# Differential attention in a two-block transformer kernel: rope from PSUM, a scaling on ScalarE, units at uneven distances

## The chip, the cores and the metric

The kernel runs on one core of a Trainium2 chip. The metric is the device time in microseconds (us); it is stated as the median of several executions. One further execution was recorded by the hardware profiler. All views of the trace below are of that execution.

## What is computed

Two transformer blocks run one after the other, in fp32, on 512 tokens of width 1024. The change touches only the even mixer of the second block, and in it the differential attention: 8 heads, each with two maps of 64 features, whose softmaxes are subtracted.

```python
def diff_attention_group(q, k, v, pos, layer, lambdas, subln):
    q = rope(q.reshape(bsz, s, 2 * hh, d), pos).reshape(bsz, s, hh, 2, d)
    k = rope(k.reshape(bsz, s, 2 * hh, d), pos).reshape(bsz, s, hh, 2, d)
    lam = jnp.exp(jnp.sum(lf[0] * lf[1])) - jnp.exp(jnp.sum(lf[2] * lf[3])) + lam_init
    scale = d ** -0.5                      # 1/8
    def block(start, q1b, q2b):            # 128 queries against all keys, chunk-causal mask
        p1 = masked_softmax(einsum('bqhd,bkhd->bhqk', q1b, k1) * scale, mask)
        p2 = masked_softmax(einsum('bqhd,bkhd->bhqk', q2b, k2) * scale, mask)
        return einsum('bhqk,bkhe->bqhe', p1 - lam * p2, vf)
    o = rms_norm(o, subln) * (1.0 - lam_init)
```

## The kernel before

**Stages.** The kernel is written by hand, engine by engine; every engine runs its instructions strictly in the order of the program and waits on semaphores. The stage of the change is `ev_qk_out`, about 1595 to 1865 us. On every engine it is a loop over 192 steps. TensorE makes in steps 0 to 127 the 16 projections of queries and keys (`ev_qk`, 8 steps each: n, k = divmod(step, 8)) and in steps 128 to 191 the first halves of the 8 output tiles (`ev_out`). Each step is one product: three matmuls of 128x512 (high x high, high x low, low x high parts of fp32), lines 939 to 941. All the other work stands between products, at steps given by functions.

**Rope.** When projection n is done, ScalarE copies it from its PSUM bank (n % 2) to `raw2` (line 2179, k = 0 of the next tile). At k = 2 TensorE exchanges its halves with a permutation matrix into bank 2 (`swap`, line 1466), and VectorE multiplies the copy by the cosines (line 2904), the exchanged one by the sines (2906) into `swp`, and adds (2907) into `qk2`; this posts `roped`.

**Units.** A unit is one head and one block of 128 queries, with 128, 256, 384 or 512 keys (i = 0 to 3): 32 units, the four of a head one after another, 4 steps apart from step 40 on (`UNIT_AT`, `UNIT_STEPS`). For the unit that starts at step s:

- s: TensorE `scores` (1477) for both maps into banks 4 and 5. VectorE `maxes`: masks a corner (2915), takes the maximum (2917), multiplies it by -1/8 (2918). ScalarE `exps` (2139), two exponentials with their sums. VectorE `weights` of the unit before: reciprocals of the sums (2925), second map times its inverse sum and -lambda (2927), first map times its inverse sum plus the second (2928). It stands in the order of the program behind `maxes` of the new unit.
- s + 8 (`TURN`): TensorE transposes the weights (`turn`, 1487) into bank 6, ScalarE copies them (2148).
- s + 11 (`MIX`): TensorE multiplies by the values (`mix`, 1497) into bank 7.

**Heads.** At `head_mixed_at(h)`, the step of the last mix, VectorE copies the head's output (2972) and ScalarE squares it (2188); the next head's first `mix` waits for that copy. Three steps on, TensorE sums the squares (`sub_sum`, 1507). After heads 3 and 7, at + 4, VectorE makes variance and reciprocal (2977, 2978) and ScalarE four roots (`sub_root`, 2156), and from `spread_at(h)` on TensorE spreads them (`sub_rows`, 1518) and VectorE scales (2982); ScalarE and VectorE split the result into high and low parts (2193, 2939). In steps 120 to 129 they also split the eight tiles of the mamba branch's y (2201, 2959).

**Beside it** GpSimd splits each weight panel, once in 16 steps, into a high part (3354, 4 pieces) and a low part (3358, 4 pieces). SyncE loads the panels and, once all 16 tiles are roped, x (line 860).

## Time and profile before

| | |
|---|---|
| median of 3 executions | 2912.23 us (2909.16 to 2913.40) |
| profiled execution | 2908.97 us |
| its span in the trace | 2907.1 us |
| busy: TensorE, VectorE, ScalarE, GpSimd | 97%, 48%, 29%, 47% of the span |
| mean granted TensorE clock | 0.988 of full |

The profile says of each engine how long it was busy, and of each instruction when it began, how long it lasted, and which instruction of another engine released it when it had stood still ahead of it. Matmuls overlap, and their ends are modelled: the distance from start to start is the measure, not the duration. Times in the trace count from the span's start.

### The profile page before, as it was taken

The page shows a single profiled execution, that of the slowest core. Times are in us where ns is not written, and L with a number is a line of the kernel's source. Part 1 is how long each engine was busy: PE and PEld are TensorE (multiplying, and loading weights), DVE is VectorE, ACT ScalarE, POOL GpSimd, SP SyncE. Part 2 cuts the span into 40 slices and gives each one's busy share as a digit, 9 for nine tenths or more (in the row PEclk, how much of TensorE's full clock was granted, in tenths as well). Part 3 has the DMA queues.
Part 4 walks back from the last instruction along what each step waited for, and adds up shares of the span by engine and source line. Part 5 has one row for each costly group of instructions (what it writes and reads, how often), then busy time and mean ns, then how long its engine had stood idle before and what let it go on. Part 6 is the DMA issues. An engine that isn't in the chain of part 4 may idle for free.

```text
span 2907.1 us, 36763 instructions
## 1 busy us (share of the span) xinstructions
PE 2810.6 (97%) x14588; PEld 2171.8 (75%) x14588; DVE 1397.8 (48%) x2266; ACT 847.4 (29%) x1575; POOL 1355.7 (47%) x1106
## 2 busy tenths in 40 slices
PE   7999999999989999999999989999999998999997
PEld 5888777777878877677886656778788755788886
DVE  3321556776573122435847777523825856511113
ACT  3011432331130133322336234232223234222222
POOL 2344323324434654558765543754544412744443
PEclk8999999999999999999999999999999999999999
DMA  7112222222321122123311112222333320323322
GB/s 269 44 44 66 66 66 95 70 70 94 131 76 59 58 73 73 62 91 122 105 61 59 58 48 69 84 94 87 102 96 90 116 64 30 126 91 89 99 85 74
DMA packets 244837, 243.81 MB, mean 84 GB/s; under 512 B 5392, under 2 KB 234640, under 8 KB 244048
## 3 DMA queue, kind: packets, MB, share of 16 engines
q1 hardware_dynamic: 243376, 237.96, 25.6%
q0 software_dynamic: 1312, 3.80, 0.5%
q8 instruction: 102, 1.67, 0.2%
q14 instruction: 47, 0.39, 0.0%
HBM read 233.22 MB, written 7.34 MB: 83 GB/s over the span
## 4 chain that ended last, share of the span: by engine, by line
PE 83%; DVE 11%; issue 2%; ACT 2%; POOL 1%; SPq 1%; DMA 1%; DVEq 0%; POOLq 0%; ACTq 0%
PE psum L939 22%; PE psum L941 21%; PE psum L940 21%; PE psum L1209 4%; PE psum L1188 1%; PE psum L1144 1%; DVE columns L2644 1%; PE psum L1164 1%; PE psum L1326 1%; PE psum L1143 1%; POOL columns L3358 1%; PE psum L1213 1%; DVE columns L2917 1%; PE psum L1477 1%; SPq L776 1%
## 5 line engine op out<-in xcount | busy, mean ns | idle before, releaser
L939 PE MATMUL psum<-columns,columns 128*128 128x512 f32 (+1 forms) x3464 | 1348.6, 389 | 13.4 <-POOL columns L3358 5.0
L941 PE MATMUL psum<-columns,columns 128*128 128x512 f32 (+1 forms) x3464 | 1263.6, 365 | 0.0
L940 PE MATMUL psum<-columns,columns 128*128 128x512 f32 (+1 forms) x3464 | 1262.5, 364 | 0.0
L3358 POOL TENSOR_TENSOR columns<-columns,columns 128x512 fp32r<-128x512 f32 (+1 forms) x676 | 912.1, 1379 | 437.8 <-ACT columns L1873 404.6
L3354 POOL TENSOR_TENSOR columns<-columns,columns 128x512 fp32r<-128x512 f32 x392 | 419.1, 1100 | 1005.7 <-PE psum L941 775.3
L939 PEld LDWEIGHTS psum<-columns,columns 128*128 128x128 f32 x3464 | 654.6, 189 | 198.9 <-issue 77.1
L940 PEld LDWEIGHTS psum<-columns,columns 128*128 128x128 f32 x3464 | 655.3, 189 | 125.7 <-issue 28.6
L941 PEld LDWEIGHTS psum<-columns,columns 128*128 128x128 f32 x3464 | 653.8, 189 | 112.5
L1873 ACT ACTIVATE columns<-columns 128x1024 fp32r<-128x1024 f32 (+2 forms) x154 | 136.8, 936 | 171.9 <-PE psum L941 166.2
L2644 DVE SCALAR_TENSOR_TENSOR columns<-columns,columns,columns 128x256 f32<-128x256 f32 x224 | 154.4, 743 | 0.0
L2626 DVE SCALAR_TENSOR_TENSOR columns<-columns,psum 128x512 f32<-128x512 f32 x80 | 54.8, 685 | 187.5 <-PE psum L1209 185.0
L3026 DVE TENSOR_TENSOR columns<-columns,psum 128x512 f32<-128x512 f32 x44 | 30.3, 689 | 207.7 <-PE psum L941 207.7
L1209 PE MATMUL psum<-columns,columns 128*128 128x512 f32 x256 | 121.2, 596 | 1.9 <-DVE columns L2603 1.9
L3020 DVE TENSOR_TENSOR columns<-psum,columns 128x512 f32<-128x512 f32 x44 | 30.3, 692 | 152.3 <-PE psum L941 152.0
L2585 DVE TENSOR_REDUCE columns<-psum 128x1 f32<-128x768 f32 (+3 forms) x80 | 61.5, 769 | 64.5 <-PE psum L1144 63.4
L3142 DVE TENSOR_TENSOR psum<-psum,columns 128x512 f32<-128x512 f32 x32 | 22.4, 700 | 129.7 <-PE psum L941 129.6
L1984 ACT ACTIVATE columns<-psum,columns 128x768 f32<-128x768 f32 (+3 forms) x80 | 59.3, 742 | 71.6 <-DVE columns L2588 71.6
L2214 ACT ACTIVATE columns<-columns 128x512 fp32r<-128x512 f32 x44 | 27.8, 633 | 179.5 <-DVE columns L3026 179.5
L1999 ACT ACTIVATE columns<-psum 128x512 f32<-128x512 f32 (+1 forms) x80 | 44.0, 550 | 113.4 <-PE psum L1164 113.4
L2025 ACT ACTIVATE columns<-psum,columns 128x512 f32<-128x512 f32 x64 | 43.6, 681 | 113.8 <-PE psum L941 113.7
L1991 ACT ACTIVATE columns<-columns,columns 128x768 f32<-128x768 f32 (+3 forms) x80 | 62.6, 783 | 46.0 <-DVE columns L2596 45.9
L2210 ACT ACTIVATE columns<-columns 128x512 f32<-128x512 f32 x44 | 27.8, 634 | 162.5 <-DVE columns L3020 162.2
(414 smaller groups left out, 2745.6 us busy)
## 6 DMA issues: line engine op xcount, KB each, us to landing
columns<-in_w_merge SPq DMA_DIRECT2D x32, 1024.0 KB, 6.7
columns<-in_w_ada SPq DMA_DIRECT2D x24, 1024.0 KB, 5.7
columns<-in_w_in SPq DMA_DIRECT2D x22, 1024.0 KB, 5.3
columns<-in_ev_w_in SPq DMA_DIRECT2D x22, 1024.0 KB, 5.2
columns<-in_ffn_gate SPq DMA_DIRECT2D x22, 1024.0 KB, 5.4
columns<-in_ffn_up SPq DMA_DIRECT2D x22, 1024.0 KB, 5.3
columns<-in_ffn_down SPq DMA_DIRECT2D x16, 768.0 KB, 4.7
columns<-in_ffn_down SPq DMA_DIRECT2D x16, 640.0 KB, 4.3
```

Of the source, the lines that this page charges most:

```text
L939: mm(dst, weights(0, k), moving(0, k), start=start and k == 0, stop=False)
L940: mm(dst, weights(0, k), moving(1, k), start=False, stop=False)
L941: last = mm(dst, weights(1, k), moving(0, k), start=False, stop=stop and k == k_tiles - 1)
L1209: last = mm(psum[:, o:o + SEQ], brs[:, n % 2, k, part * P:(part + 1) * P], gx[:, r, k, :], start=k == 0, stop=k == 1)
L1873: last = f(w_parts[0][:, (SPLITS[q] - 1) % 2, a:b], ring[:, raw_slot, a:b], ACT.Copy)
L1984: f(prob[:, u % 2, 0:n], psum[:, o:o + n], ACT.Exp, bias=cols[:, u % 2:u % 2 + 1], scale=0.125, accum_out=cols[:, 4 + u % 2:5 + u % 2]).th ...
L1991: f(prob[:, u % 2, 0:n], prob[:, u % 2, 0:n], ACT.Identity, scale=cols[:, 24 + u % 8:25 + u % 8]).then_inc(prob_weighed, 1)
L2585: order(v.tensor_reduce(top, psum[:, o:o + n], AX.X, ALU.max))
L2626: v.scalar_tensor_tensor(out=acc if j < quarter else g, in0=g, scalar=1.0, in1=y, op0=ALU.add, op1=ALU.mult).then_inc(merge_used, 1)
L2644: last = v.scalar_tensor_tensor(out=acc, in0=w, scalar=sil[:, k, b:b + 1], in1=acc, op0=ALU.mult, op1=ALU.add)
L3354: last = g.tensor_tensor(high[:, c], raw[:, c], zero.broadcast_to([P, c.stop - c.start]), ALU.add)
L3358: last = g.tensor_tensor(low[:, c], raw[:, c], high[:, c].bitcast(F32), ALU.subtract)
```

## The change

Within the stage, six things:

1. The rope's cosine product becomes `cosines`, one step after the raw copy (k = 1), and reads the projection in its PSUM bank; the swap and the rest of the rope move from k = 2 to k = 4 (`ROPE_AT`). The sine product is written back into bank 2, and the sum reads it there; the buffer `swp` goes. So a projection's bank is free for the next but one only when its tile is roped: TensorE waits for `roped` where it waited for `raw_ready`.
2. The factor 1/8 goes from the exponential into the raw copy and the cosine product, for query tiles only (`is_query`).
3. The maximum is written negated by the reduction itself; the multiplication behind it goes.
4. `weights` is parted: `inverses` (reciprocals and -lambda times that of the second map) ahead of `maxes`, and behind it the one combining instruction, which waits for ScalarE. ScalarE's new `scale` multiplies the second map by its column.
5. Units start at 0, 3, 7 and 11 of each head's 16 steps instead of 0, 4, 8 and 12, from step 40 on; ScalarE's exponentials are put 2 steps after the start in its order (`EXPS`), `turn` and `mix` stay at 8 and 11.
6. The work at a head's end moves back against `head_mixed_at`: the copy from + 0 to + 2, the square from + 0 to + 3, `sub_sum` from + 3 to + 5, variance and roots from + 4 to + 6, `sub_rows` from + 7 to + 9. `head_mixed_at(h)` itself is one step earlier.

```diff
--- before.py
+++ after.py
@@ -297,7 +297,8 @@
 V_SLOTS, Z_SLOTS, HEADS_AT = 16, 16, 12
 QK_STEPS, OUT_STEPS = 128, 64
 UNITS2 = [(h, i) for h in range(8) for i in range(4)]
-UNIT_AT, UNIT_STEPS, TURN, MIX = 40, 4, 8, 11
+UNIT_STARTS = [40 + 16 * h + (0, 3, 7, 11)[i] for h, i in UNITS2]
+ROPE_AT, EXPS, TURN, MIX, LAST_WEIGHTS = 4, 2, 8, 11, UNIT_STARTS[-1] + 5
 
 
 def qk_tile(n):
@@ -305,20 +306,24 @@
     return 2 * (n // 4) + n % 2 + 8 * (n % 4 // 2)
 
 
+def is_query(n):
+
+    return n % 4 < 2
+
+
 def unit2_at(step, phase):
 
-    u = step - UNIT_AT - phase
-    return u // UNIT_STEPS if u >= 0 and u % UNIT_STEPS == 0 and u // UNIT_STEPS < len(UNITS2) else None
+    return UNIT_STARTS.index(step - phase) if step - phase in UNIT_STARTS else None
 
 
 def head_mixed_at(h):
 
-    return UNIT_AT + UNIT_STEPS * (4 * h + 3) + MIX
+    return UNIT_STARTS[4 * h + 3] + MIX
 
 
 def spread_at(h):
 
-    return head_mixed_at(3) + 7 + 3 * h if h < 4 else head_mixed_at(7) + 7 + 2 * (h - 4)
+    return head_mixed_at(3) + 9 + 3 * h if h < 4 else head_mixed_at(7) + 9 + 2 * (h - 4)
 
 
 OD_TILES = (4, 5, 6, 7, 8, 9, 0, 1, 2, 3)
@@ -524,7 +529,7 @@
         lamw, lam_products = take(128, at=A + 19952), take(2, 64, at=A + 20080)
 
         qk2 = take(16, SEQ, at=A + 10240)
-        swp, raw2 = take(SEQ, at=4096), take(2, SEQ, at=5120)
+        raw2 = take(2, SEQ, at=5120)
         sq5, rs5 = take(2, SEQ, at=0), take(SEQ, at=2 * SEQ)
         pr_diff = (take(2, 2, SEQ, at=brs_at), take(2, SEQ, at=A + 4096))
         sub_sq, sub_rs, sub_v = take(SEQ, at=A + 5120), take(SEQ, at=A + 5120 + SEQ), take(P, at=A + 18448)
@@ -1527,10 +1532,10 @@
                         mix(u)
                     if step % 2 == 0 and 1 <= step // 2 <= KD:
                         gate_sum(step // 2 - 1)
-                    if k == 2 and 1 <= n <= 16:
+                    if k == ROPE_AT and 1 <= n <= 16:
                         swap(n - 1)
                     for h in range(8):
-                        if step == head_mixed_at(h) + 3:
+                        if step == head_mixed_at(h) + 5:
                             sub_sum(h)
                         if step == spread_at(h):
                             sub_rows(h)
@@ -1544,17 +1549,15 @@
                             if n < 2:
                                 pe.wait_ge(z_ready, 7 + n)
                             else:
-                                pe.wait_ge(raw_ready, n - 1)
+                                pe.wait_ge(roped, n - 1)
                         o, src = n % 2 * BANK, h2_parts
                     else:
                         t = n - 16
                         if k == 0:
                             if t % 2 == 0:
                                 w = split_ready(PANEL0["ev_out"] + t // 2)
-                            if t < 2:
-                                pe.wait_ge(raw_ready, 15 + t)
-                            elif t == 2:
-                                pe.wait_ge(roped, 16)
+                            if t < 3:
+                                pe.wait_ge(roped, min(15 + t, 16))
                             else:
                                 pe.wait_ge(half_added, t - 2)
                         if t == 0:
@@ -2136,9 +2139,15 @@
                         act.wait_ge(turned2, u - 1)
                     for a in range(2):
                         o, c = (4 + a) * BANK, 2 * (u % 2) + a
-                        last = f(pr_diff[0][:, u % 2, a, 0:n], psum[:, o:o + n], ACT.Exp, bias=cols[:, c:c + 1], scale=0.125,
+                        last = f(pr_diff[0][:, u % 2, a, 0:n], psum[:, o:o + n], ACT.Exp, bias=cols[:, c:c + 1],
                                  accum_out=cols[:, 4 + c:5 + c])
                     last.then_inc(p2_ready, 1)
+
+                def scale(u):
+                    n = (UNITS2[u][1] + 1) * P
+                    p = pr_diff[0][:, u % 2, 1, 0:n]
+                    act.wait_ge(total_inverted, UNITS0[2] + u + 1)
+                    f(p, p, ACT.Identity, scale=cols[:, 5 + 2 * (u % 2):6 + 2 * (u % 2)]).then_inc(prob_weighed, 1)
 
                 def copy(u):
                     n = (UNITS2[u][1] + 1) * P
@@ -2158,6 +2167,11 @@
 
                 for step in range(QK_STEPS + OUT_STEPS):
                     n, k = divmod(step, 8)
+                    u = unit2_at(step, 0)
+                    if u:
+                        scale(u - 1)
+                    if step == LAST_WEIGHTS:
+                        scale(len(UNITS2) - 1)
                     u = unit2_at(step, TURN)
                     if u is not None:
                         copy(u)
@@ -2176,17 +2190,17 @@
                         act.wait_ge(gemm_done, JOB0["ev_qk"] + i + 1)
                         if i >= 2:
                             act.wait_ge(roped, i - 1)
-                        f(raw2[:, i % 2, :], psum[:, i % 2 * BANK:(i % 2 + 1) * BANK], ACT.Copy).then_inc(raw_ready, 1)
-                    u = unit2_at(step, 0)
+                        f(raw2[:, i % 2, :], psum[:, i % 2 * BANK:(i % 2 + 1) * BANK], ACT.Copy, scale=0.125 if is_query(i) else 1.0).then_inc(raw_ready, 1)
+                    u = unit2_at(step, EXPS)
                     if u is not None:
                         exps(u)
                     for h in range(8):
-                        if step == head_mixed_at(h):
+                        if step == head_mixed_at(h) + 3:
                             act.wait_ge(o2_used, h + 1)
                             if h:
                                 act.wait_ge(sub_summed, h)
                             f(sub_sq, qk2[:, h, :], ACT.Square).then_inc(sub_squared, 1)
-                        if h % 4 == 3 and step == head_mixed_at(h) + 4:
+                        if h % 4 == 3 and step == head_mixed_at(h) + 6:
                             sub_root(h // 4)
                         if step == spread_at(h) + 1:
                             act.wait_ge(sub_scaled, h + 1)
@@ -2898,13 +2912,16 @@
 
             def ev_qk_out():
 
+                def cosines(n):
+                    dve.wait_ge(raw_ready, n + 1)
+                    order(v.scalar_tensor_tensor(out=qk2[:, qk_tile(n), :], in0=psum[:, n % 2 * BANK:(n % 2 + 1) * BANK],
+                                                 scalar=0.125 if is_query(n) else 1.0, in1=cosd, op0=ALU.mult, op1=ALU.mult))
+
                 def rope(n):
-                    x = qk2[:, qk_tile(n), :]
-                    dve.wait_ge(raw_ready, n + 1)
-                    v.tensor_tensor(x, raw2[:, n % 2, :], cosd, ALU.mult)
+                    x, swp = qk2[:, qk_tile(n), :], psum[:, 2 * BANK:3 * BANK]
                     dve.wait_ge(swapped, n + 1)
-                    order(v.tensor_tensor(swp, psum[:, 2 * BANK:3 * BANK], sind, ALU.mult))
-                    v.tensor_tensor(x, x, swp, ALU.add).then_inc(roped, 1)
+                    order(v.tensor_tensor(swp, swp, sind, ALU.mult))
+                    v.tensor_tensor(x, swp, x, ALU.add).then_inc(roped, 1)
                     dve.wait_ge(roped, n + 1)
 
                 def maxes(u):
@@ -2914,17 +2931,20 @@
 
                     order(v.memset(s[0:64, :, n - 64:n], NEG))
                     c = cols[:, 2 * (u % 2):2 * (u % 2) + 2]
-                    order(v.tensor_reduce(c, s[:, :, 0:n], AX.X, ALU.max))
-                    v.tensor_scalar(c, c, -0.125, None, ALU.mult).then_inc(maxed2, 1)
-
-                def weights(u):
-
-                    n = (UNITS2[u][1] + 1) * P
+                    v.tensor_reduce(c, s[:, :, 0:n], AX.X, ALU.max, negate=True).then_inc(maxed2, 1)
+
+                def inverses(u):
                     c = cols[:, 4 + 2 * (u % 2):6 + 2 * (u % 2)]
                     dve.wait_ge(p2_ready, u + 1)
                     order(v.reciprocal(c, c))
+                    v.tensor_scalar(c[:, 1:2], c[:, 1:2], lamw[:, 5:6], None, ALU.mult).then_inc(total_inverted, 1)
+
+                def weights(u):
+
+                    n = (UNITS2[u][1] + 1) * P
+                    c = cols[:, 4 + 2 * (u % 2):6 + 2 * (u % 2)]
                     p = pr_diff[0][:, u % 2, :, 0:n]
-                    order(v.tensor_scalar(p[:, 1], p[:, 1], c[:, 1:2], lamw[:, 5:6], ALU.mult, ALU.mult))
+                    dve.wait_ge(prob_weighed, UNITS0[2] + u + 1)
                     v.scalar_tensor_tensor(out=p[:, 0], in0=p[:, 0], scalar=c[:, 0:1], in1=p[:, 1], op0=ALU.mult, op1=ALU.add)\
                         .then_inc(p2_weighted, 1)
 
@@ -2957,20 +2977,25 @@
                         i = step - QK_STEPS + KD - 2
                         dve.wait_ge(y_high, i + 1)
                         v.tensor_tensor(y_parts[1][:, i, :], xbc[:, i, :], y_parts[0][:, i, :].bitcast(F32), ALU.subtract).then_inc(y_split, 1)
-                    if k == 2 and 1 <= n <= 16:
+                    if k == 1 and 1 <= n <= 16:
+                        cosines(n - 1)
+                    if k == ROPE_AT and 1 <= n <= 16:
                         rope(n - 1)
                     u = unit2_at(step, 0)
                     if u is not None:
+                        if u:
+                            inverses(u - 1)
                         maxes(u)
                         if u:
                             weights(u - 1)
-                    if step == UNIT_AT + UNIT_STEPS * len(UNITS2):
+                    if step == LAST_WEIGHTS:
+                        inverses(len(UNITS2) - 1)
                         weights(len(UNITS2) - 1)
                     for h in range(8):
-                        if step == head_mixed_at(h):
+                        if step == head_mixed_at(h) + 2:
                             dve.wait_ge(mixed2, 4 * h + 4)
                             v.tensor_copy(qk2[:, h, :], psum[:, 7 * BANK:8 * BANK]).then_inc(o2_used, 1)
-                        if h % 4 == 3 and step == head_mixed_at(h) + 4:
+                        if h % 4 == 3 and step == head_mixed_at(h) + 6:
                             dve.wait_ge(sub_summed, h + 1)
                             if h == 7:
                                 dve.wait_ge(sub_std, 1)
```

## Rows read from the trace of the kernel before

**Rows 1.** The page, part 1: busy us, share of the span, instructions.
```profile
PE 2810.6 (97%) x14588; PEld 2171.8 (75%) x14588; DVE 1397.8 (48%) x2266; ACT 847.4 (29%) x1575; POOL 1355.7 (47%) x1106
```

**Rows 2.** TensorE's waits, 1590 to 1860 us: total us, times, longest.
```profile
PE psum L1487 <- DVE columns L2928: 12.4, 13, 2.1
PE psum L1518 <- ACT columns L2156: 2.9, 1, 2.9
...
PE psum L1477 <- ACT columns L2139: 1.2, 1, 1.2
PE psum L1466 <- ACT columns L2179: 1.1, 1, 1.1
```

**Rows 3.** TensorE in time: start, us, instruction, [idle before it, releaser].
```profile
1708.98 0.27 PE L1487 MATMUL psum<-columns,columns 128*128 128x128 f32 x1
1709.18 0.92 PE L1477 MATMUL psum<-columns 64*128 64x384 f32 x4
...
1714.31 0.40 PE L941 MATMUL psum<-columns,columns 128*128 128x512 f32 x1
1714.95 0.44 PE L1487 MATMUL psum<-columns,columns 128*128 128x128 f32 x2 [0.24 <-DVE columns L2928]
...
1721.29 0.55 PE L1487 MATMUL psum<-columns,columns 128*128 128x128 f32 x3 [1.42 <-DVE columns L2928]
...
1731.56 0.27 PE L1487 MATMUL psum<-columns,columns 128*128 128x128 f32 x1
...
1769.88 0.33 PE L1487 MATMUL psum<-columns,columns 128*128 128x128 f32 x1 [2.10 <-DVE columns L2928]
```

**Rows 4.** VectorE and GpSimd in time, 1709 to 1720 us.
```profile
1709.22 4.03 POOL L3354 TENSOR_TENSOR columns<-columns,columns 128x512 fp32r<-128x512 f32 x4 [12.38 <-PE psum L941]
...
1710.40 0.96 DVE L2917 TENSOR_REDUCE columns<-psum 128x2 f32<-128x768 f32 x1
1711.39 0.89 DVE L2918 TENSOR_SCALAR columns<-columns 128x2 f32<-128x2 f32 x1
...
1713.33 6.09 POOL L3358 TENSOR_TENSOR columns<-columns,columns 128x512 fp32r<-128x512 f32 x4
...
1713.43 1.46 DVE L2928 SCALAR_TENSOR_TENSOR columns<-columns,columns 128x256 f32<-128x256 f32 x1
```

**Rows 5.** By line: ns least/median/most, first and last start, forms.
```profile
L2904 DVE TENSOR_TENSOR columns<-columns,columns x16: 679/688/1753, 1602.6 to 1771.4; 128x512 f32<-128x512 f32 x16
L2906 DVE TENSOR_TENSOR columns<-psum,columns x16: 677/680/692, 1605.9 to 1772.0; 128x512 f32<-128x512 f32 x16
L2907 DVE TENSOR_TENSOR columns<-columns,columns x16: 691/868/1339, 1606.6 to 1772.7; 128x512 f32<-128x512 f32 x16
L2918 DVE TENSOR_SCALAR columns<-columns x32: 169/170/1065, 1636.1 to 1815.7; 128x2 f32<-128x2 f32 x32
L2928 DVE SCALAR_TENSOR_TENSOR columns<-columns,columns x32: 351/684/1465, 1640.5 to 1818.5; 128x128 f32<-128x128 f32 x8, 128x256 f32<-128x256 f32 x8, 128x384 f32<-128x384 f32 x8, 128x512 f32<-128x512 f32 x8
```

**Rows 6.** ScalarE: group of 1040 to 1250 us by shape; one square in time.
```profile
L1991 ACT ACTIVATE columns<-columns,columns 128x512 f32<-128x512 f32 x5 | 3.6, 720 | 0.1
...
1709.21 0.63 ACT L2188 ACTIVATE columns<-columns 128x512 f32<-128x512 f32 x1 [1.62 <-DVE columns L2972]
```

**Rows 7.** The roots of the first four heads, in time.
```profile
1741.23 0.95 DVE L2978 RECIPROCAL columns<-columns 128x128 f32<-128x128 f32 x1
1742.21 1.26 ACT L2156 ACTIVATE columns<-columns 32x128 f32<-32x128 f32 x4 [4.78 <-DVE columns L2978]
1743.53 2.07 PE L1518 MATMUL psum<-columns,columns 128*128 128x512 f32 x2 [2.89 <-ACT columns L2156]
```

**Rows 8.** Two stretches: us, busy us (instructions) by engine, granted clock, DMA.
```profile
1743.50:1747.00 3.50, 3.47 (x8) 2.15 (x9) 2.20 (x6) 3.47 (x7) 0.00 (x0) 0.52 0.83 286
...
1770.20:1773.70 3.50, 3.50 (x11) 1.82 (x10) 3.36 (x5) 0.39 (x1) 0.76 (x1) 0.58 0.00 0
```

**Rows 9.** VectorE in time: a scaling with one operand in PSUM.
```profile
1751.11 0.74 DVE L2982 SCALAR_TENSOR_TENSOR columns<-columns,columns,psum 128x512 f32<-128x512 f32 x1
```

4 lines of the change are left out of this document (2 added, 2 removed).

## Prediction

> **What bounds the kernel now.** Read the page's first part before anything else: TensorE is busy for 97% of the span, every other engine for under half of it [rows 1]. So an edit on VectorE or ScalarE can only give back time in which TensorE stood still in this stage, and the next view is TensorE's waits over the stage (1590 to 1860 us), line by line [rows 2]. The largest is line 1487, the transposes of `turn`, which waited for line 2928, the last instruction of `weights` on VectorE: 12.4 us in 13 waits. Three single waits follow: 2.9 us of `sub_rows` (1518), 1.2 us of `scores` (1477), 1.1 us of `swap` (1466).
>
> Third view, TensorE in order of time through one head [rows 3]. Matmuls of 512 columns start about 0.23 us apart and are modelled to last 0.40, so the real loss of a wait is its idle time plus about 0.17: the last product before a turn started at 1714.31, the turn at 1714.95 instead of 1714.54. The same two turns are late in each head: that of the second unit (0.24 here) and that of the third (1.42). One head (first turn to first turn, 1708.98 to 1731.56) takes 22.6 us, of which (0.24 + 0.17) + (1.42 + 0.17) = 2.0 is waiting. 20.6 us is TensorE's own work and stays.
>
> Why is `weights` late? Between 1709 and 1722 GpSimd splits the next weight panel, 4 pieces of 1.0 us and then 4 of 1.5 [rows 4]. In that burst the 2-column negation 2918 took 0.89 us against a median of 0.17, and the 256-column line 2928 took 1.46, more than the 0.684 median over all widths. By line over the whole stage [rows 5]: 2904 and 2907, both of whose inputs lie in SBUF, range from 0.68 to 1.75 and from 0.69 to 1.34; 2906, which reads PSUM, is 0.677 to 0.692 in all 16 cases. This is the part of VectorE's time that the change goes at.
>
> **The clock.** The granted clock averaged 0.52 and 0.58 of full in two stretches of 3.5 us [rows 8], that is mostly at the lower of its two levels, 1.2 instead of 2.4 GHz. The first began as the 2.89 us wait of 1518 ended [rows 7], the second after the 2.10 us wait at 1769.88 [rows 3]. Each costs 3.5 x (1 - 0.52) = 1.7 and 3.5 x (1 - 0.58) = 1.5 us. Waits of 1.42 us are not followed by one.
>
> **All that can be won**: turns 12.4 + 13 x 0.17 = 14.6; `sub_rows` 3.1; `swap` 1.3; `scores` 1.4; clock 3.2. Together 23.6 us.
>
> **Part by part.** *Rope reads PSUM.* Today 2904 + 2906 + 2907 are 0.69 + 0.68 + 0.87 by the medians and 1.75 + 0.68 + 1.07 where they fall into the burst. `cosines` becomes a scalar_tensor_tensor with one PSUM operand; the nearest row is 2982, 0.74 [rows 9]. The other two read and write a PSUM bank; nearest 2906, 0.68. In-place PSUM output isn't shown among my rows: from below 0.68, from above 0.87 (2907), I take 0.69. New sum 2.1 us, the same in and out of the burst: 0.1 to 1.4 us less of VectorE per tile, 16 tiles. `cosines` also waits for the raw copy, so two engines never read the bank together; the bank is now free only when the tile after it is roped. That is the wait `roped` at k = 0 on TensorE: rope of tile n-2 stands at step 8(n-1)+4, four steps (4 x 0.7 = 2.8 us and more with the unit work) ahead. I cost it at nothing; if VectorE were over 3 us late at that point it would appear.
> *Scale in the copy and in `cosines`*: immediates of instructions that are there anyway, nothing.
> *Negated maximum*: removes 32 x 2918 (0.17, up to 1.07 in the burst), 12 us of VectorE, directly on the chain scores, maximum, exponential.
> *Second map scaled on ScalarE*: VectorE loses 32 x 2927 and keeps the reciprocal, plus a one-column multiplication that can wait for a GpSimd piece like 2918 did (0.17 to 1.07). ScalarE gets 32 scalings; the same operation with a column as scale stands in the first block, line 1991, 0.72 us at 512 columns [rows 6], so some 2 us per head on an engine with 29% load [rows 1]. Behind it in ScalarE's queue are the copy of the transposes and the raw copy; both have a step or more of room. VectorE waits for it in `weights`, but runs `maxes` in between, which hides it.
> *Starts at 0, 3, 7, 11 of 16 steps, swap at k = 4.* `weights(u)` still stands at the next unit's start. Second unit: its turn now comes 4 steps after, and the rope, 2.2 to 3.5 us of VectorE, no longer stands in between. Third unit: 4 steps, the rope behind `weights`. I laid the rows out for one head (scores of the third unit start at t = 0): scores to end of the maximum takes from 1709.18 to 1711.36, 2.2 us [rows 3, 4]; `weights` of the second unit then waits up to 1.0 for a GpSimd piece and takes about 0.5, done by 3.3 to 3.7; its turn comes at scores 0.92 + four products of 0.70 (three matmuls 0.23 apart) + the first unit's turn 0.20 = 3.9 [rows 3]. Cleared, with 0.2 to 0.6 to spare. In the same way the third unit's turn has over 1 us, the fourth's over 1. So the 14.6 us of the turns go.
>
> **What is late next.** *The head's sum of squares.* In program order VectorE copies the last head's output after `weights` of the second unit (0.68), ScalarE squares it (0.63 [rows 6]), and `sub_sum` stands on TensorE right behind this turn and the mix: t = 3.9 + 0.4 (two transposes, rows 3's 0.44) + 0.2 (one matmul of 128 columns, like one transpose) = 4.5. The chain gives 3.4 + 0.68 + 0.63 + 0.1 for the hand-over = 4.8. New wait about 0.3 per head, bounds 0 (weights meets no piece) and 1.0 (it meets a piece of 1.5). Five ordinary heads: 1.5 us (0 to 5).
> *Head 5* (steps 120 to 135) has the eight low halves of y (two SBUF inputs, 0.68 to 1.75 like 2904) and two of the four 0.74 us subnorm scalings ahead of that copy. Extra 0.68 to 1.5 + 0.74, plus about 1 us of backlog: `mix` and `sub_sum` wait 1.6 to 4, I take 2.5. Before, this stretch lost 1.3 + 2.3.
> *Head 6*: the low half of head 3 now lies just ahead of the copy (step 144 both), in the burst: 0.5 + 0.68 more, 1.5 us in all.
> *Group root*: `sub_sum` to `sub_rows` is 4 steps as before; rope, the 0.95 us reciprocal and the 1.26 us of roots [rows 7] still come one after another, and now the fourth unit's exponentials queue behind the roots with a table load. I find 1.6 to 2.4 us at `sub_rows` and 1.1 at the next `scores`: 3.1, unchanged, and so is its low clock, 1.7.
> *First scores*: one step less between the first two units, but a rope that is 1 us shorter: 1.4, unchanged (0.5 to 2.5).
> *Second stretch of low clock*: its waits shrink from 3.6 to about 2.5; half a chance, 0.8.
> Sum lost after: 1.5 + 2.5 + 1.5 + 3.1 + 1.7 + 1.4 + 0.8 = 12.5. Gain 23.6 - 12.5 = **11.1 us**. The reload of x (waits for the last rope) and the weight panels follow TensorE and have room; the rest of the kernel runs the same.
>
> **A rule weighed against the rows.** Line 2906 never felt the GpSimd burst, 2904 and 2918 did [rows 5]. The Trainium skill (SBUF — State Buffer, Who interferes with whom) says that a VectorE instruction contends with GpSimd when it has two SBUF inputs or is in a two-port mode, which tensor_scalar can enter, and not with at most one SBUF input outside those modes. By that rule, the trace agrees for the parts removed, but it also speaks against the change: `weights` keeps two SBUF inputs and the small multiplication in `inverses` is a tensor_scalar, so both stay exposed.
>
> **Rivals.** (1) *All goes*: the root and both low-clock stretches as well, new waits near nothing; only the first scores stay and some 2 us. For it: VectorE gets some 3 us per head free. Against it: the root's chain is as long. Gain 17 to 22 us, about 2893. Chance 0.12. (2) *Turns stay partly late*: the 0.2 to 0.6 us of the second unit is thin; if `weights` misses it by 0.7 in each head, 8 x 0.7 = 5.6 come back, and gain is 3 to 7, about 2907. Chance 0.17 (0.07 of it still beyond 0.2%). (3) *The new waits eat it*: `sub_sum` at its bound of 1.0 in five heads, head 5 at 4 with its low clock: 5 + 4 + 1.5 (head 6) + 1.5 (clock) + 4.8 (root with its clock) + 1.4 = 18.2, a gain of 5.4 at the most and less with any turn late: about 2909 and no change that can be told. Chance 0.10. (4) *Slower*: ScalarE and VectorE now wait for each other twice per unit in program order. If the copy of the head's output with its square falls behind a GpSimd piece of 1.5 us and the late scaling, `mix` and `sub_sum` wait over 2.5 us in each of 7 heads, 17 us, and each such wait may bring a low clock of 1.5. It decides from (23.6 - 9.5) / 7 = 2.0 us per head, where 9.5 is root 4.8, first scores 1.4, clock 0.8 and 2.5 for what heads 5 and 6 have extra; at 3.0, with one more low clock, 7 x 3.0 + 9.5 + 1.5 - 23.6 = 8.4 us more, 2921. Against it: I find 0.3. Chance 0.06. (5) That ScalarE would reload its table for the scaling (1.28 us twice per unit, which would fill ScalarE) is excluded: line 1991 alternates with exponentials in a window whose groups hold no table load [rows 6]; it has no share of its own.
>
> **Numbers.** The profiled execution took 2908.97 us (span 2907.1); the median of the three is 2912.23, 3.3 above it. The gain belongs to the stage, so I take it from the median: 2912.2 - 11.1 = 2901.1. Forecast case 0.55, gain 7 to 16. A measurement of this kernel tells about 0.2%, 5.8 us, from no change. Faster: 0.55 + 0.12 + 0.07 = 0.74; same: 0.10 + 0.10 = 0.20; slower 0.06. The range takes in the forecast case and rivals 1 and 2: 2912 - 22 = 2890 to 2912 - 3 = 2909; it leaves out 0.16.
>
> **What would show it.** Right: 1487's wait on `weights` falls under 2 us in all; 16 ropes of 2.1 us with hardly a spread; reductions with no 2-column instruction behind them; head period 20.6 to 21.2; a new wait on the square (1507) or the copied output (1497) of some 0.3 per head. Wrong: turns still late in the second or third unit; waits at k = 0 of a tile for the rope; `sub_rows` with no wait, or several new stretches of low clock.

## The result, and the profile after

The changed kernel takes 2892.65 us (median of 6; 2891.02 to 2897.56) against 2909.61 us before (median of 6), a ratio of 0.9944 with a 95% interval of 0.9934 to 0.9955. The forecast was 2901.1 within 2890 to 2909, so 11 us were expected and 17 came. One of the ten timed executions of e6 below took 4597.10 us at a mean granted clock of 0.554, and is left out of its ratio. The profiled execution took 2892.76 us, its span 2890.9 us, 16.2 less than before.

For the comparisons below I use a second measure beside the ratio, the length of the stage in the trace: from TensorE's first wait in it (for ScalarE's squares, line 1460 before, 1465 after) to the first product behind the 192 steps. Before it ran from 1594.85 to 1841.07 us, 246.2 us; after from 1593.33 to 1823.54, 230.2. So 16.0 of the 16.2 us lie in the stage. A stage comes from one profiled execution of a kernel, a ratio from several timed ones.

After, the view of [rows 2], TensorE's waits in the stage (waiting line, releaser, total us, times, longest), is:

```profile
PE psum L1502 <- DVE columns L2997: 3.2, 2, 2.0
PE psum L1523 <- ACT columns L2165: 2.5, 1, 2.5
PE psum L1465 <- ACT columns L2184: 2.0, 1, 2.0
PE psum L1482 <- ACT columns L2142: 1.2, 2, 1.0
...
PE psum L944 <- DVE columns L2924: 0.4, 1, 0.4
```

The line of the turns (1492 now) is not in the list at all: its 13 waits and 12.4 us are gone. New is 1502, `mix`, which waits for VectorE's copy of a head's output, twice. `sub_rows` (1523) still waits, 2.5 us against 2.9, and behind it `scores` (1482) for the exponentials. TensorE in order of time shows both, and that a head takes 20.4 us from first turn to first turn, where [rows 3] gave 22.6:

```profile
1659.98 0.27 PE L1492 MATMUL psum<-columns,columns 128*128 128x128 f32 x1
...
1680.42 0.27 PE L1492 MATMUL psum<-columns,columns 128*128 128x128 f32 x1
...
1703.85 0.43 PE L1512 MATMUL psum<-columns,columns 128*32 128x128 f32 x8
...
1732.86 1.13 PE L1523 MATMUL psum<-columns,columns 128*128 128x512 f32 x2 [2.49 <-ACT columns L2165]
...
1735.71 0.49 PE L1482 MATMUL psum<-columns 64*128 64x128 f32 x4 [1.03 <-ACT columns L2142]
...
1753.65 0.46 PE L1502 MATMUL psum<-columns,columns 128*128 128x128 f32 x2 [1.97 <-DVE columns L2997]
...
1774.78 0.46 PE L1502 MATMUL psum<-columns,columns 128*128 128x128 f32 x2 [1.27 <-DVE columns L2997]
```

By line, as in [rows 5] (ns least/median/most): the cosine product (2917), the sine product in its bank (2923), the sum (2924), the one-column multiplication (2940), the combination (2948), and ScalarE's scaling (2150):

```profile
L2917 DVE SCALAR_TENSOR_TENSOR columns<-psum,columns x16: 673/682/692, 1601.1 to 1755.0; 128x512 f32<-128x512 f32 x16
...
L2923 DVE TENSOR_TENSOR psum<-psum,columns x16: 686/697/700, 1606.6 to 1759.0; 128x512 f32<-128x512 f32 x16
...
L2924 DVE TENSOR_TENSOR columns<-psum,columns x16: 691/692/693, 1607.4 to 1759.7; 128x512 f32<-128x512 f32 x16
...
L2940 DVE TENSOR_SCALAR columns<-columns,columns x32: 212/214/216, 1634.1 to 1798.8; 128x1 f32<-128x1 f32 x32
...
L2948 DVE SCALAR_TENSOR_TENSOR columns<-columns,columns x32: 341/876/1666, 1635.5 to 1800.5; 128x128 f32<-128x128 f32 x8, 128x256 f32<-128x256 f32 x8, 128x384 f32<-128x384 f32 x8, 128x512 f32<-128x512 f32 x8
...
L2150 ACT ACTIVATE columns<-columns,columns x32: 401/562/725, 1634.3 to 1799.8; 128x128 f32<-128x128 f32 x8, 128x256 f32<-128x256 f32 x8, 128x384 f32<-128x384 f32 x8, 128x512 f32<-128x512 f32 x8
```

A rope is 0.68 + 0.70 + 0.69 = 2.07 us in all 16 cases, within 0.02 each, in and out of GpSimd's burst. The combination still feels the burst (0.34 to 1.67), more than 2928 did (median 0.876 against 0.684): 17 of its 32 cases start while a piece of a split runs, where it was 8. No stretch of low clock lies in the stage any more; before there were the two of [rows 8], together 6.8 us. The stretch right behind the root's waits, where the first of them lay, is now at the full clock (1.00, third from the end):

```profile
1735.00:1740.00 5.00, 4.29 (x23) 3.29 (x24) 3.56 (x8) 4.41 (x12) 0.00 (x0) 1.00 0.11 35
```

### The profile page after: what moved, and what is told of

Same layout as the page of the kernel before. It is cut to its first block, busy times and chain, and to the rows that moved or that the text cites. A ratio compares the mean times of both kernels' runs of the same rounds, so it can differ in the third digit from the quotient of the medians.

```text
span 2890.9 us, 36778 instructions
## 1 busy us (share of the span) xinstructions
PE 2805.8 (97%) x14588; PEld 2174.3 (75%) x14588; DVE 1363.5 (47%) x2234; ACT 863.6 (30%) x1607; POOL 1351.7 (47%) x1106
## 3 DMA queue, kind: packets, MB, share of 16 engines
q8 instruction: 102, 1.67, 0.2%
## 4 chain that ended last, share of the span: by engine, by line
PE 83%; DVE 11%; ACT 2%; issue 2%; POOL 1%; SPq 1%; DMA 0%; DVEq 0%; POOLq 0%; ACTq 0%
PE psum L944 22%; PE psum L946 21%; PE psum L945 21%; PE psum L1214 4%; PE psum L1193 1%; PE psum L1149 1%; DVE columns L2658 1%; PE psum L1169 1%; PE psum L1482 1%; PE psum L1148 1%; PE psum L1331 1%; POOL columns L3383 1%; PE psum L1218 1%; PE psum L1502 1%; SPq L781 1%
```

## The experiments

Two theories were set against each other. V: what made the turns late was VectorE's chain in GpSimd's burst; each thing taken off it brings the turns forward by as much. D: the distances between units and the later swap make the room, the savings on VectorE matter little. The first four kernels carry one part each, then parts are undone and orders moved. All results are in one table. Each ratio is to the kernel before, timed beside it. "Low clock" is the time in the stage at the lower level, by the trace. The last column is an estimate: the stage less half of that time, since the lower level is 1.2 instead of 2.4 GHz. It takes off a little too much where TensorE was waiting anyway. It is needed because the low clock does not follow the edits alone. In e3 and e9 one stretch of 3.4 us (from 1595.27, from 1593.98) lies at the very start of the stage, behind the 2.0 us wait for the squares that all 14 traces have, and ahead of all that these kernels change.

| kernel | ratio to before, 95% | stage, us | TensorE waits for `weights`, us | low clock, us | stage less half of it, us (estimate) |
|---|---|---|---|---|---|
| before | 1 | 246.2 | 12.4 | 6.8 | 242.8 |
| the change | 0.9944 (0.9934 to 0.9955) | 230.2 | 0 | 0 | 230.2 |
| e1 rope only | 0.9967 (0.9958 to 0.9977) | 236.8 | 6.9 | 3.4 | 235.1 |
| e2 negated maximum only | 0.9961 (0.9947 to 0.9975) | 236.8 | 8.9 | 0 | 236.8 |
| e3 scaling on ScalarE only | 0.9985 (0.9975 to 0.9995) | 241.6 | 1.7 | 6.8 | 238.2 |
| e4 distances only | 1.0043 (1.0026 to 1.0060) | 258.8 | 12.3 | 20.5 | 248.5 |
| e5 the change at even distances | 0.9933 (0.9917 to 0.9950) | 227.6 | 0 | 6.8 | 224.2 |
| e6 the change, scaling on VectorE | 1.0013 (1.0000 to 1.0027) | 245.7 | 6.3 | 6.8 | 242.3 |
| e7 the change, copy earlier | 0.9928 (0.9911 to 0.9945) | 226.8 | 0 | 0 | 226.8 |
| e8 e7 with the roots reordered | 0.9944 (0.9927 to 0.9961) | 230.2 | 0.9 | 6.8 | 226.8 |
| e9 e5, square later | 0.9954 (0.9940 to 0.9968) | 233.8 | 0 | 6.8 | 230.4 |
| e10 the change again | 0.9941 (0.9927 to 0.9955) | 230.2 | 0 | 0 | 230.2 |
| e11 e5, scaling on VectorE | 0.9938 (0.9924 to 0.9951) | 230.0 | 4.4 | 0 | 230.0 |
| e12 e5, copy first | 0.9933 (0.9920 to 0.9947) | 225.8 | 0 | 3.4 | 224.1 |

### One part at a time

**e1**, the rope alone, at k = 2 as before (TensorE's wait for the bank moves to `roped` with it):

```diff
-                    v.tensor_tensor(x, raw2[:, n % 2, :], cosd, ALU.mult)
+                    swp = psum[:, 2 * BANK:3 * BANK]
+                    order(v.scalar_tensor_tensor(out=x, in0=psum[:, n % 2 * BANK:(n % 2 + 1) * BANK],
+                                                 scalar=1.0, in1=cosd, op0=ALU.mult, op1=ALU.mult))
                     dve.wait_ge(swapped, n + 1)
-                    order(v.tensor_tensor(swp, psum[:, 2 * BANK:3 * BANK], sind, ALU.mult))
-                    v.tensor_tensor(x, x, swp, ALU.add).then_inc(roped, 1)
+                    order(v.tensor_tensor(swp, swp, sind, ALU.mult))
+                    v.tensor_tensor(x, swp, x, ALU.add).then_inc(roped, 1)
```

> Only the rope is changed against the kernel before: the cosine product reads the projection's PSUM bank, the sine product stays in bank 2; swap and rope stay at k = 2. Theory V (VectorE's chain in the GpSimd burst is what makes the turns late): the rope goes from 3.4 us in the burst to 2.1, so the third unit's turn, 1.42 us late in each head, is at most 0.2 us late, the second unit's 0.25 stays; waits of the turns 12.4 -> 3 to 5 us, time 7 to 10 us less. Theory D (the distances of the units make the room, the savings on VectorE matter little): turns wait 10 to 12.4 us as before, time within 3 us.

```profile
PE psum L1487 <- DVE columns L2928: 6.9, 10, 2.1
```

The third unit's turn, late by 1.42 us in heads 0 to 3 before, isn't late any more in heads 0 to 4. The second unit's wait stays, 0.9 in head 0 and 0.24 to 0.34 in heads 1 to 4. That is as theory V has it. The total of the turns fell only to 6.9, not to 3 to 5, because heads 5 to 7 keep all of theirs: 2.1, 0.2, 1.2, 0.4 and 1.1. The stage is 9.4 us shorter, 7.7 of them without the low clock.

**e2**, the maximum negated by the reduction, the factor 1/8 in the raw copy:

```diff
-                    order(v.tensor_reduce(c, s[:, :, 0:n], AX.X, ALU.max))
-                    v.tensor_scalar(c, c, -0.125, None, ALU.mult).then_inc(maxed2, 1)
+                    v.tensor_reduce(c, s[:, :, 0:n], AX.X, ALU.max, negate=True).then_inc(maxed2, 1)
```

> Only the maximum is taken negated by the reduction, with the factor 1/8 in the raw copy, against the kernel before. Theory V: 0.9 us less in the second unit of each head and 0.9 to 1.0 less ahead of the third: second unit's wait gone, third's 1.42 -> 0.4, waits of the turns 12.4 -> 3 to 5 us, time 6 to 9 us less. Theory D: turns wait 10 to 12.4 us, time within 3 us.

The second unit's wait is gone in ordinary heads, as V says. The third's is 0.9 to 1.0 in heads 1 to 3 (1.3 in head 0) and not 0.4, so leaving out the 2-column instruction is worth about 0.5 there. The time is 3.9 parts in a thousand less (11 us; I had 6 to 9), though the waits of the turns fell by 3.5 only. The 6.8 us of low clock went as well; without it the stage is 6.0 us shorter. The third unit's turn in head 3, the fourth head:

```profile
1714.74 0.55 PE L1492 MATMUL psum<-columns,columns 128*128 128x128 f32 x3 [0.88 <-DVE columns L2932]
```

**e3**, `inverses` and ScalarE's `scale` alone, at even distances:

```diff
+                def scale(u):
...
+                    act.wait_ge(total_inverted, UNITS0[2] + u + 1)
+                    f(p, p, ACT.Identity, scale=cols[:, 5 + 2 * (u % 2):6 + 2 * (u % 2)]).then_inc(prob_weighed, 1)
...
+                    u = unit2_at(step, 0)
+                    if u:
+                        scale(u - 1)
...
```

> Only the second map is scaled on ScalarE (inverses ahead of maxes) against the kernel before. Theory V: VectorE is spared 1.0 us in the second unit and 0.5 in the third and pays back up to 0.2 for the small multiplication: waits of the turns 12.4 -> 1 to 4 us, time 8 to 12 us less. Theory D: turns wait 10 us or more, time within 3 us, or slower where VectorE stands waiting for ScalarE's scaling (line 1 of weights released by ScalarE, over 5 us in all).

Neither quite. The turns came right (1.7 us left), but the gain was half of what I expected from that, 4 us and not 8 to 12. TensorE's waits show where most of it went:

```profile
PE psum L1477 <- ACT columns L2139: 4.9, 9, 1.2
PE psum L1466 <- ACT columns L2190: 2.9, 1, 2.9
```

`scores` now wait for the exponentials of the unit before, 9 times, mostly 0.5 us, and one swap waits 2.9 for the raw copy. ScalarE's scaling waits for VectorE's inverses (0.5 us ahead of the scaling at 1720.01, 1.4 ahead of that at 1760.72, with the raw copy behind it), and whatever stands behind it in ScalarE's order waits too.

**e4**, the uneven starts, the swap at k = 4 and the later end of a head alone, parts 1 to 4 undone in the changed kernel:

```diff
+UNIT_STARTS = [40 + 16 * h + (0, 3, 7, 11)[i] for h, i in UNITS2]
+ROPE_AT, EXPS, TURN, MIX, LAST_WEIGHTS = 4, 2, 8, 11, UNIT_STARTS[-1] + 5
```

> Only the uneven starts, the swap at k = 4 and the later work at a head's end against the kernel before; cosines from the copy in SBUF stand at k = 1. Theory V: the third unit's wait goes, since the rope is behind weights now, but the second's turn comes 3.9 us after its successor's scores and weights are done after 5.6: it is 1.2 to 1.7 us late in each head, and the copy of the head's output behind it holds mix and the sum of squares: time within 3 us of before, or up to 10 us slower. Theory D: turns no longer wait (under 2 us), time 8 us or more less.

```profile
1691.44 0.44 PE L1492 MATMUL psum<-columns,columns 128*128 128x128 f32 x2 [1.39 <-DVE columns L2933]
1692.14 0.46 PE L1502 MATMUL psum<-columns,columns 128*128 128x128 f32 x2 [0.26 <-DVE columns L2979]
...
1714.28 0.44 PE L1492 MATMUL psum<-columns,columns 128*128 128x128 f32 x2 [1.30 <-DVE columns L2933]
```

Theory D falls. The wait moved from the third unit to the second, 1.3 to 1.4 us in each head, with `mix` waiting for the copied output right behind it in seven of them. The kernel is 12.5 us slower by ratio (0.0043 x 2910), and the stage 12.6 longer; that is past my bound of 10. Over half of it is the clock: 20.5 us of the stage lie at the lower level against 6.8 before, and without that the stage is 5.7 us longer. One stretch of it, by engine and with the granted clock (0.50) third from the end:

```profile
1750.00:1755.00 5.00, 4.31 (x14) 3.17 (x14) 3.02 (x9) 3.77 (x13) 0.00 (x0) 0.50 0.00 0
```

### Undoing one part of the change

**e6**, the change with the second map scaled in `weights` again:

```diff
-                    dve.wait_ge(prob_weighed, UNITS0[2] + u + 1)
...
+                    dve.wait_ge(p2_ready, u + 1)
+                    order(v.reciprocal(c, c))
...
+                    order(v.tensor_scalar(p[:, 1], p[:, 1], c[:, 1:2], lamw[:, 5:6], ALU.mult, ALU.mult))
```

> The changed kernel with one part undone: the second map is scaled on VectorE again, in weights. Theory V2: with uneven distances the second unit's turn comes 3.9 us after the next scores; maximum 2.2, reciprocal 0.2, scaling 1.0 and combination 1.5 in the burst are 4.8 us: its turn waits 0.8 to 1.2 us in each of 8 heads, and the copied output with mix another 0.3: 9 to 12 us of the 17 are lost, ratio 0.997 to 0.999. Rival (the scaling's place does not matter, rope and negation do it): turns wait under 2 us, ratio 0.993 to 0.996.

The direction is V's, and the loss larger: the whole gain is gone. The second unit is late by 0.3 to 0.4 us, not by 0.8 to 1.2, but the third is late as well, 0.46 in heads 1 to 4, which I had not foreseen, `mix` waits 5.3 us for the copied output and `sub_rows` 3.4. So at uneven distances the scaling on ScalarE is worth 15.5 us of stage (12.1 without the low clock). The trace is of one of e6's shorter executions (2908.63 us); by the ratios of e6 and the change it is 0.0069 x 2910 = 20 us.

**e5**, the change with its distances, its swap and its head's end put back (`cosines` stays at k = 1):

```diff
-UNIT_STARTS = [40 + 16 * h + (0, 3, 7, 11)[i] for h, i in UNITS2]
-ROPE_AT, EXPS, TURN, MIX, LAST_WEIGHTS = 4, 2, 8, 11, UNIT_STARTS[-1] + 5
+UNIT_STARTS = [40 + 16 * h + (0, 4, 8, 12)[i] for h, i in UNITS2]
+ROPE_AT, EXPS, TURN, MIX, LAST_WEIGHTS = 2, 0, 8, 11, UNIT_STARTS[-1] + 4
...
```

> The changed kernel with its distances undone: units every 4 steps, swap at k = 2, exponentials and the work at a head's end where they were; rope from PSUM, negated maximum and scaling on ScalarE stay. Theory V2 (the uneven distances are worth something only because ScalarE's scaling stands ahead of the exponentials): no turn waits for VectorE (under 1 us in all), but scores wait for the exponentials about 0.5 us per head, 3 to 5 us in all, and mix no longer waits for the copied output (3.2 us in the changed kernel): ratio to before 0.994 to 0.9965. Rival (the distances carry the gain once VectorE is relieved): turns of the second or third unit wait 5 us or more, ratio over 0.997.

Better than either line of the expectation: no turn waits, no copy, no `sub_rows`, and `scores` once, for 0.4 us. With the shorter rope and no negation on VectorE the 4.9 us that `scores` waited in e3 have shrunk to 0.4. One large wait is left, of the last swap, and 6.8 us of low clock begin within it, at 1749.93:

```profile
1732.86 0.49 PE L1482 MATMUL psum<-columns 64*128 64x128 f32 x4 [0.42 <-ACT columns L2142]
1750.62 2.07 PE L1471 MATMUL psum<-columns,columns 128*128 128x512 f32 x2 [2.69 <-ACT columns L2193]
```

**e11**, e5 with the scaling back on VectorE, so the rope from PSUM and the negated maximum with its factor 1/8 alone (parts 1 to 3 of the list, the swap at k = 2):

```diff
                 def weights(u):
...
-                    dve.wait_ge(prob_weighed, UNITS0[2] + u + 1)
...
+                    dve.wait_ge(p2_ready, u + 1)
+                    order(v.reciprocal(c, c))
+                    order(v.tensor_scalar(p[:, 1], p[:, 1], c[:, 1:2], lamw[:, 5:6], ALU.mult, ALU.mult))
...
-                        if u:
-                            inverses(u - 1)
```

> Even distances, rope from PSUM and negated maximum, the second map scaled on VectorE as before. If savings on VectorE add up until the turns are on time and nothing after that, this kernel gives most of the gain: the second unit's 0.25 us (left by the rope alone) goes with the negation, turns wait under 2 us in all: ratio 0.993 to 0.9955. If ScalarE's scaling carries part of the gain at even distances: ratio over 0.996.

```profile
PE psum L1492 <- DVE columns L2933: 4.4, 5, 1.6
```

The ratio is that of the whole change. The turns wait 4.4 us, more than the 2 I gave, in five places: 0.6 in head 0 and 0.9, 1.6, 0.9 and 0.5 in heads 5 to 7. Heads 1 to 4 have none. **e10**, the change again beside it, not one line changed:

> The changed kernel again, on the same chip as e9 and e11. If its uneven distances are worth nothing once the three parts are in, it is not faster than e9 and e5: ratio 0.994 to 0.995 as on its first timing.

Its trace repeats that of the change: the same waits within 0.01 us, a stage of 230.2, no low clock. So two of the ideas, rope and negation, bring what the whole change brings (230.0 against 230.2 us of stage; 0.9938 and 0.9941, intervals on each other). At even distances ScalarE's scaling takes 2.4 us more off the stage (e5 against e11), and the distances cost 2.6 us of stage on top of the three (the change against e5). Neither can be told from nothing by the timed ratios. The low clock hides part of both: e5 has 6.8 us of it in the stage and the two others none, so without it the differences would be 5.8 and 6.0 us.

### The waits that were left

**e7**: the copy of a head's output one step earlier and ahead of the unit.

```diff
+                    for h in range(8):
+                        if step == head_mixed_at(h) + 1:
+                            dve.wait_ge(mixed2, 4 * h + 4)
+                            v.tensor_copy(qk2[:, h, :], psum[:, 7 * BANK:8 * BANK]).then_inc(o2_used, 1)
                     u = unit2_at(step, 0)
```

> The changed kernel with VectorE's copy of a head's output one step earlier and ahead of that step's unit, so also ahead of the low halves and the scaling of heads 5 and 6. If the two waits of mix (2.0 and 1.3 us) come from what stands ahead of the copy in VectorE's order, they go and nothing takes their place: 3 to 3.5 us less than the changed kernel, ratio to before 0.993. If VectorE is simply overloaded there, turns or scores wait by as much instead: ratio 0.994 to 0.9945 as the changed kernel.

The order was the cause: both waits of `mix` are gone and the stage is 3.4 us shorter. Something did take their place, though, in head 5:

```profile
1750.40 0.42 PE L1512 MATMUL psum<-columns,columns 128*32 128x128 f32 x8 [2.27 <-ACT columns L2202]
```

The sum of squares waits 2.3 us for the square, which on ScalarE stands behind the high part of another head's output. `sub_rows` waits 1.4 instead of 2.5, which I had not expected of this edit. The trace shows where it comes from: the combination ahead of the rope and the root takes 0.61 us, where in the changed kernel it took 1.65. There it started at 1727.21, just behind the start of a piece of the split (1727.17), and ended after that piece. In e7 it starts at 1724.49, just ahead of a piece (1724.57), and goes through; the piece is the longer one instead (1.69 us, the one before it 1.28). Changed kernel first, then e7:

```profile
1727.21 1.65 DVE L2948 SCALAR_TENSOR_TENSOR columns<-columns,columns 128x384 f32<-128x384 f32 x1
...
1724.49 0.61 DVE L2948 SCALAR_TENSOR_TENSOR columns<-columns,columns 128x384 f32<-128x384 f32 x1
```

**e8**: in addition, for head 3, variance and reciprocal ahead of the rope, and the roots behind the fourth unit's exponentials (`sub_root` at + 7).

```diff
-                        if h % 4 == 3 and step == head_mixed_at(h) + 6:
+                        if h % 4 == 3 and step == head_mixed_at(h) + (7 if h == 3 else 6):
                             sub_root(h // 4)
...
+                    for h in (3, 7):
+                        if step == head_mixed_at(h) + 6:
+                            dve.wait_ge(sub_summed, h + 1)
...
+                            v.reciprocal(sub_v, sub_v).then_inc(sub_var, 1)
                     if k == ROPE_AT and 1 <= n <= 16:
```

> The same, and for the first four heads variance and reciprocal ahead of the rope on VectorE, the fourth unit's exponentials ahead of the roots on ScalarE. Expected: sub_rows waits 1.0 us instead of 2.5 and the next scores not at all instead of 1.0: 2 to 3 us less than with the copy alone, ratio 0.992 to 0.9925. Rival: the roots then wait for two table loads behind the exponentials and sub_rows waits 2.5 us or more: no gain over the copy alone.

`sub_rows` waits 1.0 and the next `scores` no longer (0.4 one unit on), as expected, and the kernel is not faster than the change. The time came back in head 5: a turn late by 0.9, the sum of squares by 2.6, and 6.8 us of low clock, without which the stage is as long as that of e7. The late turn is again one combination beside a split, 1.17 us where the same one took 0.48 in e7. In e7 it starts 0.12 us ahead of a piece (1746.71), in e8 0.15 behind the start of one (1746.46). First e7, then e8:

```profile
1746.59 0.48 DVE L2948 SCALAR_TENSOR_TENSOR columns<-columns,columns 128x256 f32<-128x256 f32 x1
...
1746.61 1.17 DVE L2948 SCALAR_TENSOR_TENSOR columns<-columns,columns 128x256 f32<-128x256 f32 x1
```

So a tenth of a us in the order of arrival is worth 0.7 to 1.0 us of one instruction here.

**e9**: e5 with ScalarE's square one step later, behind the raw copy.

```diff
-                        if step == head_mixed_at(h):
+                        if step == head_mixed_at(h) + 1:
                             act.wait_ge(o2_used, h + 1)
```

> The kernel of e5 (the change with its even distances kept) with one move: ScalarE's square of a head's output one step later, behind that step's raw copy. In e5 the swap of the last tile waited 2.7 us, because on ScalarE the square waited for VectorE's copy and held the high part of y, and with it VectorE's inverses, the scaling and the raw copy; a stretch of 6.8 us of low clock followed. If that chain is the cause, the wait goes (under 0.5 us) and the low clock with it: 3 to 6 us less than e5, ratio to before 0.991 to 0.9925. If VectorE's load in this head is the cause, a wait of 2 us or more stays at swap or a turn: ratio as e5, 0.9933.

A miss: 6.2 us of stage worse than e5. The swap's wait went from 2.7 to 1.7 only, and the sum of squares, three steps behind the last mix, waited in each of seven heads:

```profile
PE psum L1512 <- ACT columns L2202: 6.8, 7, 1.5
```

The prediction's rival of a slower kernel rested on a late square in seven heads. Here the square is late by its place in ScalarE's order, and costs 0.66 us in the first four of them and 1.2 to 1.5 in the last three, not the 2.5 and more of the rival. Its low clock is no more than e5's; half of it lies at the stage's start.

**e12**: e5 with VectorE's copy first in its step instead.

```diff
+                    for h in range(8):
+                        if step == head_mixed_at(h):
+                            dve.wait_ge(mixed2, 4 * h + 4)
+                            v.tensor_copy(qk2[:, h, :], psum[:, 7 * BANK:8 * BANK]).then_inc(o2_used, 1)
                     if QK_STEPS - KD + 1 < step <= QK_STEPS + 1:
...
-                        if step == head_mixed_at(h):
-                            dve.wait_ge(mixed2, 4 * h + 4)
-                            v.tensor_copy(qk2[:, h, :], psum[:, 7 * BANK:8 * BANK]).then_inc(o2_used, 1)
```

> The kernel of e5 with one move: VectorE's copy of a head's output first in its step, ahead of the scaling of the subnorm and the low half of y; in the other heads its place is the same. In e5 the chain copy, square, high part, low part, inverses, scaling, raw copy ended in a 2.7 us wait of the last swap. With the copy 2.1 us earlier the rest comes 1.3 to 1.6 us earlier: swap waits 1.0 to 1.4 us. If the low clock of 6.8 us behind that wait goes too, 4 to 5 us less than e5, ratio 0.9915 to 0.9925; if it stays, 1.5 us less, 0.9928. Rival (VectorE is overloaded there, and any order gives the wait back elsewhere): ratio as e5, 0.9933, and 2.5 us or more of waits in that head.

The shortest stage of all, 225.8 us; the swap waits 2.1 and not 1.0 to 1.4, and half of e5's low clock remains. Without the low clock it is as long as e5's (224.1 against 224.2 us). By the timed ratio (0.9933) it is no different from e5, and neither can be told from the change.

## Why the prediction came out as it did

**The number**: right in direction and inside the range, by the range's width and not by the sum. 17.0 us came where the sum gave 11.1; the forecast case was drawn from 7 to 16, and 17 is the foot of rival 1 (*all goes*, 17 to 22), which had a chance of 0.12. What happened lies between the two: both stretches of low clock went, as in the rival, while the root's waits stayed and heads 5 and 6 got new ones, as in the forecast case. The figure 2901.1 is off by 8.5 us, of which 2.6 are the kernel before, whose median is now 2909.61 and not 2912.23.

**Where the time is lost**: right. TensorE's own work per head was put at 20.6 us and is 20.4, with a small wait still in it (below). All 16 us came out of TensorE's waits and low clock in this stage.

**Prices**: the three parts of the rope were put at 0.74 + 0.68 + 0.69 and are 0.68 + 0.70 + 0.69, so in-place output in PSUM (0.70) costs hardly more than output to SBUF (0.69); ScalarE's scaling at 512 columns was 0.72 and is up to 0.725. The one-column multiplication was priced at 0.17 to 1.07 and is 0.21 in all 32 cases, 15 of them begun while a piece of a split ran. So the exposure that I derived from the rule for it did not come; for the combination it did.

**The turns**: 14.6 us were to go, and went.

**What is late next**, term by term (idle in the trace + 0.17 each):

| term of the sum lost after | predicted, us | measured, us |
|---|---|---|
| `sub_sum` in five ordinary heads | 1.5 | 0.8 (see below) |
| head 5 | 2.5 | 2.1 |
| head 6 | 1.5 | 1.4 |
| root, `sub_rows` and next `scores` | 3.1 | 2.7 + 1.2 = 3.9 |
| low clock behind the root | 1.7 | 0 |
| first scores | 1.4 | 0.4, and 0.6 at the product for the rope |
| second low clock | 0.8 | 0 |
| sum | 12.5 | 9.2 |

23.6 - 9.2 = 14.4, and the stage gave 16.0. The gain was forecast 5.9 us short, 11.1 against 17.0 between the medians. 3.3 of them are this table: 2.5 too much for the low clock, 0.7 for the sum of squares, 0.9 for heads 5 and 6 and the first scores, and 0.8 too little at the root. 1.6 are the stage's gain beyond the terms, which my estimates from start to start leave open (it would be 2.1 but for the idle of 0.78 us ahead of the first product behind the steps, where it was 0.31 before, a loss in none of my terms). 1.0 is what the medians show beyond the stage.

The sum of squares is no wait in the list, which counts idle time from 0.15 us on, and yet the predicted wait is there. VectorE and ScalarE in order of time, one ordinary head:

```profile
1701.42 1.11 DVE L2948 SCALAR_TENSOR_TENSOR columns<-columns,columns 128x256 f32<-128x256 f32 x1
...
1702.46 0.68 DVE L2997 COPY columns<-psum 128x512 f32<-128x512 f32 x1
...
1703.17 0.63 ACT L2202 ACTIVATE columns<-columns 128x512 f32<-128x512 f32 x1
```

The chain is the one I laid out. It ended at 1703.80, and TensorE started at 1703.85 (line 1512 above), released by it. In seven heads the sum starts within 0.06 us of the square's end, 0.35 to 0.39 us behind the last matmul of `mix`. Where it waits for nothing (heads 5 and 6 of e7) the distance is 0.205. So some 0.15 to 0.18 us are lost per head, where I had 0.3, and 0.8 in the first five. e9 shows what a step of difference there costs.

**The low clock** was the term of the sum that was most wrong, 2.5 us predicted and 0 measured: I left it where the root's wait is. The waits of 2.49 and 1.03 us are there in the changed kernel, and no low clock follows, in two profiled executions (the change and e10). Across the runs it came with single waits of 2.69 (e5) and 2.14 us (e12), but not with 2.27 (e7) nor 2.54 (e2), and with the 2.0 us at the stage's start in two traces of 14. No length of wait separates them, and what does stays open.

**What the reasoning did not ask.** I took the six edits as one design and costed the uneven distances as part of what brings the turns on time. e5 and e11 show that they are not: with rope and negation the turns of heads 1 to 4 are on time at even distances, and the uneven ones use up what the scaling on ScalarE frees (2.6 and 2.4 us of stage). Had I costed each edit by itself against the 1.42 and 0.25 us of [rows 3], the rope's 1.4 in the burst and the negation's 0.9 would have been seen to cover both, though e2 then measured only 0.5 for the negation in the third unit. Of the rivals, that of turns partly late did not come about: no turn waited. Of the signs listed for a right forecast, the 0.3 us per head at the square came at about half that.

## What to carry to other kernels

When TensorE is the bound and waits for one instruction of another engine, cost each edit alone against that wait; edits that only move the waiting unit, like e4, can hand the wait to its neighbour and lose. Here a VectorE operand that stayed in PSUM made the instruction's time steady beside a busy GpSimd (0.67 to 0.70 us in all cases, against up to 1.75 with both inputs in SBUF), and that steadiness was all of its worth: in a quiet stretch the cosine product took the same 0.68 us from either source. After a chain is shortened, look at what stands behind it in the order of each engine: a copy that stood too late in VectorE's order cost the changed kernel two waits, and its stage is 3.4 us shorter with it moved (e7). And before two traces are compared by a few us, take the low clock out of both.

## What the runs showed of the hardware

- A tensor_scalar on one column with a column operand took 212 to 216 ns in all 32 cases, 15 of them begun while a piece of GpSimd's splits ran. On two columns with an immediate it took 169 to 170 ns in the 21 cases outside the pieces and 340 to 1065 in the 11 begun within one. The Trainium skill (SBUF — State Buffer, Who interferes with whom) counts tensor_scalar among those that can take the shared ports. The two-column form agrees, the one-column form did not contend. The column operands are not the reason: line 2927 before has two of them and 128 to 512 columns, and took 1.02 to 1.26 us in its 8 cases within a piece against 0.35 to 0.55 outside. Whether the single column is, no run isolates.
- A reduction that negates its result takes what the plain one takes (424/824/1226 against 424/825/1225 ns).
- A combination (both inputs in SBUF) that started 0.08 and 0.12 us ahead of a piece of the split took 0.61 and 0.48 us, the same ones 0.04 and 0.15 behind the start of a piece 1.65 and 1.17 (the change, e7 and e8).
- The granted clock fell in the stage for 0 to 20.5 us in kernels that differ by a few waits, which is up to 10 us of time (an estimate, half of 20.5). Between e5 and the change, 6.8 us of low clock against none, it is worth some 3.4 us by the same estimate, more than the 2.6 us by which their stages differ.
